# Eight transposed first tiles at both feed-forward openings, and a later convolution LayerNorm schedule

## The reference

```python
for l in range(2):
    h = rmsnorm(x, mix_norm_g[l])
    # layer 0: a, gate, p = split(h @ w_in)
    #   ya = silu(layernorm(depthwise_conv31(a * sigmoid(gate)) + b))
    #   yb = multi-scale pooling mixer of p
    # layer 1: Fourier mixer (2-D DFT) beside a gated spatial mixer
    x = x + mixer_l(h) @ w_out[l]
    h = rmsnorm(x, ffn_norm_g[l])
    x = x + (silu(h @ w_gate[l]) * (h @ w_up[l])) @ w_down[l]   # hidden width 2816
out = rmsnorm(x, final_norm_g)
```

## Time and profile before

| what | value |
|---|---|
| median of 3 runs | 2642.21 us (2639.93 to 2644.13) |
| profiled execution: span of the slowest core (core 4) | 2639.2 us |
| spans of the 8 cores in it | 2633.3 to 2639.2 us |
| busy share in the span, PE / DVE / ACT / POOL | 97% / 32% / 24% / 15% |
| mean granted TensorE clock, core 4 | 0.985 |

### The profile page before, as it was taken

One profiled execution on the slowest core, in us unless ns is written; L12 is line 12 of the kernel. 1 busy time (PEld: TensorE's weight loads), 2 busy tenths in 40 slices (PEclk: granted clock), 3 DMA queues, 4 the chain that ended last, 5 costly groups with the idle time before them and its releaser, 6 DMA issues.

```text
span 2639.2 us, 38782 instructions; the slowest of 8 cores (2633.3 to 2639.2 us)
## 1 busy us (share of the span) xinstructions
PE 2549.2 (97%) x12907; PEld 1205.6 (46%) x12907; DVE 835.2 (32%) x1278; ACT 626.3 (24%) x1090; POOL 404.1 (15%) x701
## 2 busy tenths in 40 slices
PE   6999799999999999999999997999999999999998
PEld 3447344444444444444444473444444444444443
DVE  3426443222222222221223673222222222222122
ACT  3434443122111111111132353121121111111111
POOL 2200132101110111011023531221011111100100
PEclk8999899999999999999999988999999999999999
DMA  7976579856664896455564157895366447644422
GB/s 172 233 159 141 132 130 185 157 152 128 125 139 127 141 160 147 122 79 81 144 122 120 17 91 170 143 172 108 114 130 124 112 112 136 117 116 104 74 47 96
DMA packets 324877, 335.09 MB, mean 127 GB/s; under 512 B 152768, under 2 KB 282704, under 8 KB 324560
## 3 DMA queue, kind: packets, MB, share of 16 engines
q0 software_dynamic: 122096, 118.40, 32.6%
q1 hardware_dynamic: 192944, 205.30, 27.9%
q10 hardware_dynamic: 9648, 8.92, 1.2%
HBM read 331.92 MB, written 83.89 MB: 158 GB/s over the span
## 4 chain that ended last, share of the span: by engine, by line
PE 91%; DMA 3%; DVE 2%; issue 1%; SPq 1%; POOL 1%; ACT 1%; DVEq 0%; POOLq 0%; ACTq 0%
PE ps L171 91%; SPq L185 1%; DMA BIG<-hbp 1%; DMA pdr<-pst 1%; DMA w_in<-ev_w_in 1%; DMA xin<-x 0%; DMA xres<-xr 0%; DVE vt L1184 0%; POOL rs L373 0%; POOL vn L1189 0%; DVE bst L1169 0%; DMA BIG<-hb 0%; DVE bst L855 0%; DVE mv L1172 0%; ACT vn L875 0%
## 5 line engine op out<-in xcount | busy, mean ns | idle before, releaser
L171 PE MATMUL ps<-BIG,wgu 128*128 128x512 bf16 x5632 | 1229.7, 380 | 15.4 <-DMA BIG<-hbp 15.4
L171 PEld LDWEIGHTS ps<-BIG,wgu 128*128 128x128 bf16 x5632 | 551.4, 98 | 680.7 <-issue 20.9
L171 PE MATMUL ps<-wd,gT 128*128 128x512 bf16 x2816 | 609.1, 379 | 0.0
L510 DVE TENSOR_TENSOR gT<-tmp,ps 128x512 bf16<-128x512 f32 x352 | 242.1, 688 | 838.7 <-PE ps L171 792.7
L171 PEld LDWEIGHTS ps<-wd,gT 128*128 128x128 bf16 x2816 | 275.5, 98 | 332.3
L508 ACT ACTIVATE tmp<-ps 128x512 f32<-128x512 f32 x352 | 208.9, 594 | 756.8 <-PE ps L171 724.5
L171 PE MATMUL ps<-w_in,BIG 128*128 128x512 bf16 (+1 forms) x1344 | 289.2, 375 | 8.0 <-ACT pst L422 4.7
L185 POOL DMA_DIRECT2D wgu<-ffn_wgu x176 | 134.5, 765 | 855.1 <-PE ps L171 826.5
L171 PE MATMUL ps<-w_out,BIG 128*128 128x512 bf16 x1024 | 233.2, 382 | 3.6 <-ACT BIG L902 1.5
L387 ACT ACTIVATE hb<-xr 128x1024 bf16<-128x1024 f32 x80 | 84.6, 1057 | 554.7 <-DVE xr L484 280.1
L171 PEld LDWEIGHTS ps<-w_in,BIG 128*128 128x128 bf16 x1344 | 132.0, 99 | 151.6 <-issue 14.7
(11 more groups left out here) (130 smaller groups left out, 1103.1 us busy)
## 6 DMA issues: line engine op xcount, KB each, us to landing
wgu<-ffn_wgu POOLq DMA_DIRECT2D x176, 512.0 KB, 7.1
xr<-xr SPq DMA_DIRECT2D x59, 512.0 KB, 4.0
xin<-x SPq DMA_DIRECT2D x32, 512.0 KB, 6.3
xr<-xres SPq DMA_DIRECT2D x32, 512.0 KB, 5.2
xnat<-xr SPq DMA_DIRECT2D x32, 512.0 KB, 3.7
out<-xr SPq DMA_DIRECT2D x31, 512.0 KB, 2.9
xr<-x SPq DMA_DIRECT2D x28, 512.0 KB, 7.6
xres<-xr SPq DMA_DIRECT2D x28, 512.0 KB, 5.1
```

The source lines that it names most:

```text
L171: ins = self.nc.tensor.matmul(o, lhsT=l, rhs=r, start=st, stop=sp)
L510: k.op(dve, lambda e: e.tensor_tensor(out=gT[:, j, tg * 512:(tg + 1) * 512], in0=tmp[:], in1=ps[:, bl[1], :], op=ALU.mult), reads=[d_tmp, ...
```

## The change

In `prologue`, the DMA transposes of tiles 0 to 2 go. All eight tiles go through `tr_pe`, each two tiles behind its projection: tiles 0 to 4 in the loop, tiles 5 to 7 before `up(0, 0)`, `up(1, 0)` and `up(2, 0)`. In layer 0 (`npre` is 2) the copies of tiles 1 and 3 are made on VectorE behind the residual add; the others, and all in layer 1, on ScalarE ahead of it. The loop also does tile 7's projection and add, and the scaling of tile 6. `pro` does nothing after a slice any more. `feed(99)` comes before `up(3, 0)`, at the same place in the order of the instructions as before.

In `bg0`, groups 4 to 7 get one part per slice and one group per two slices: stat at j = 1, 3, 5, 7, norm at j = 2, 4, 6, 8, silu at j = 3, 5, 7, 9. Before, group 4+n had stat and norm at j = n and silu at j = n+1. Groups 8 to 11 come one slice earlier (stat at 3, 5, 7, 9; norm at 4, 6, 8, 10). At an even slice the norm of group 8+n comes before the norm of group 5+n.

```diff
                 if t + len(op.xr.s) < 8:
                     op.load(t + len(op.xr.s))
-                if t < 3:
-                    op.nrm.tr(t)
-
-            for i in range(7):
+
+            for i in range(8):
                 op.mm(i, 1 if i < npre else None)
-                if i >= 5:
+                late = npre and i % 2
+                if 2 <= i < 7 and not late:
                     op.nrm.tr_pe(i - 2, ident, d_ident, 0)
                 op.add(i)
+                if 2 <= i < 7 and late:
+                    op.nrm.tr_pe(i - 2, ident, d_ident, 1)
                 if i:
                     scale(i - 1)
                 feed(i)
 
             def pro(j, after):
-                if not after:
-                    if j < 2:
-                        scale(6 + j)
+                if after:
                     return
+                if j == 0:
+                    scale(7)
                 if j < 3:
                     op.nrm.tr_pe(5 + j, ident, d_ident, 0)
-                if j == 0:
-                    op.mm(7)
-                    op.add(7)
-                if j == 2:
+                if j == 3:
                     feed(99)
                     op.xr = xr
@@
             for n in range(4):
-                if j == n:
+                if j == 2 * n + 3:
+                    ln_silu(4 + n)
+                if j == 2 * n + 2:
+                    ln_norm(4 + n)
+                if j == 2 * n + 4:
+                    ln_norm(8 + n)
+                if j == 2 * n + 1:
                     ln_stat(4 + n)
-                    ln_norm(4 + n)
-                if j == n + 1:
-                    ln_silu(4 + n)
-                if j == 2 * n + 4:
+                if j == 2 * n + 3:
                     ln_stat(8 + n)
-                if j == 2 * n + 5:
-                    ln_norm(8 + n)
```

## The result

The changed kernel takes 2610.94 us (median of 4 runs, 2608.98 to 2613.34), against 2642.21 us for the kernel before on the same chip. The ratio is 0.988, 95% interval 0.9864 to 0.9895. Forecast was 2613.0 us, range 2606 to 2621. The gain is about 31 us where 29 were forecast.

The account below looks back on a forecast made before the run. TensorE, 91% of the chain, bounds the kernel, so only its idling can be gained. 10.1 + 14.3 + 5.6 = 30.0 us, less 0.6, off 2639.2 us, plus 3.0 to the median: 2612.8, rounded to 2613 us; range 2606 to 2621.

Parts of the forecast that it names:

- Layer 0's opening: Tile 2's projection to `up(3, 0)`: 45.1 us falls to 35.0 us if nothing waits, saving 10.1 us.
- near miss: Layer 0's tiles copied on VectorE: scaling ends just as the next projection ends; put at nothing, up to 1 us.
- Layer 1's opening: First projection to `up(3, 0)`: 55.8 us falls to 41.5 us, saving 14.3 us.
- The LayerNorm groups: After `up(3, 0)` in layer 0: 6.5 us lost now, 0.3 us back at each of three slices, saving 5.6 us.
- PSUM rotation: PSUM pairs in layer 0's opening: each pair's last reader finishes 3 us or more early; three more pairs keep phase.
- From the span to the time: Whole kernel: 0.6 us off the gain for another core ending last, 3.0 us added from span to median.
- SP's queue: Layer 0's opening: tile 7's load there at 309 to 313, add due at 311; expected loss 0, worst about 1 us.
- B: Rival, chance 0.11: ScalarE and VectorE bound the opening, 6 us come back, 2619 us.
- C: Rival, chance 0.08: the LayerNorm wait moves to silu at slices 5, 7 and 9, up to 6.5 us; 2619 us.
- D: Rival, chance 0.03: crowded transfers, landings grow from 10 to 16 us, first slices wait 5 us per layer; 2623 us.
- E: Rival, chance 0.03: slower, TensorE granted 1.2 GHz throughout both openings, their 76.5 us of work doubles; 2689 us.

Follow-up runs that it names:

- l1_only: The kernel before with the new opening in layer 1 alone, layer 0 and the LayerNorm groups as before; ratio 0.9947 against the kernel before, 14.0 us.
- norm_swap: The changed kernel with the two LayerNorm passes of group 5+n put before the four of group 8+n at the even slices; ratio 0.988 against the kernel before.
- norm_late: The changed kernel with the LayerNorm passes of groups 8 to 11 one slice later (slices 5, 7, 9, 11); 2610.55 us.
- all_act: The changed kernel with the copies of tiles 1 and 3 in layer 0 on ScalarE ahead of the add too; 2611.28 us.

## Why the prediction was right, and where it wasn't

- **Layer 0's opening**, forecast 10.1 us, measured 9.6 on core 4. The missing half is 0.35 us ahead of tile 4's transposes and rounded unit prices. It is the near miss that the step had named, VectorE's 3.7 us against TensorE's 3.9 us, and had put at nothing.
- **Layer 1's opening**, forecast 14.3, measured 14.2 on core 4, and 14.0 by time alone. Counting work between two marks that exist on both sides gave it, including the part that comes from the clock. Core 4 had one of the long openings, and the median core gained 11.2 us. Taking the terms from the slowest core fits a metric that is the slowest core, though no step of mine argued that. (The 14.4 us in the expectation of `l1_only` took the group shown as x47 at its shown start.)
- **The LayerNorm groups**, forecast 5.6, measured 5.2 on core 4, and 6.1 (3 to 9) by time. The delays at three slices came to 1.3 us, where the step had 0.9. The cause I gave (silu's transposes wait for the last pass) is not what ends last, as `norm_swap` and `norm_late` show: the same queue on ScalarE also holds the bank of the next slice.
- **PSUM rotation**: the step said that three more pairs keep the rotation over three pairs in phase. That is true up to layer 1's start, where eight banks are used again and the phase is not kept. It was worth 1.5 us, by luck in our favour. This is the step that failed, and with it the sum would have been 2611.3 us.
- **From the span to the time**: the profiled span was forecast as 2609.8 us and came out as 2609.3. The 0.6 us for another core ending last was needed: core 4 fell to 2608.1 us, and core 2 ended last, 1.2 us above it. The 3.0 us from span to median were too much. The median is 1.6 us above the profiled span, and in each of the four runs the time is 1.3 to 1.5 us above the span of its slowest core. The rest of the 3.0 us was that the profiled execution of before was a short one. So of the 1.9 us by which 2610.94 lies under 2612.8, 1.4 come from this term.
- **SP's queue**: on core 4 tile 7's load was issued at 301.36, when tile 2's store had landed, and landed 8.2 us later, at 309.6. The add ran at 311.27. That is within the 309 to 313 of the step. On core 6 the load took 10.4 us and was late. VectorE's timeline, then PE's:

```profile
312.74 1.22 DVE L484 TENSOR_TENSOR xr<-xr,ps 128x1024 f32<-128x1024 f32 x1 [3.29 <-DMA xr<-x]
```

```profile
315.52 0.61 PE L171 MATMUL ps<-ident,hbp 128*128 128x128 bf16 x8 [0.52 <-ACT hbp L387]
```

The add came about 1.5 us late, and TensorE waited ahead of tile 6's transposes, so that this core's opening is 0.7 us longer than the others'. The step had said that 1.3 us would be covered, and at worst 1 us lost.

- **The rivals**: B fell with the waits in the openings (0.35 us, and 0.7 us more on core 6) and with `all_act`. C fell with 1.3 us in all at silu. D fell too: the first weights did land later (below), but PE has no wait for `wgu`, and the late `xr` cost 0.7 us on one core. E fell with clock 1.00 and 3.62 us per group.

## What to carry to other kernels

Where the chain leaves the bounding engine for a queue, price the stretch as a whole: take two marks that exist before and after, add up the bounding engine's work between them, and what is left is the most that a change which leaves this work as it is can give there. Do it on every core, since the slowest core may not be a typical one. Here the third DMA transpose at the head of a stage kept TensorE waiting 8.4 and 7.0 us on core 4, while a tile's transposes on TensorE, two tiles behind, cost 0.45 us and little more. When a change adds or removes PSUM allocations, follow the rotation to the next place where the number of banks changes, even a thousand microseconds on.

## What was not expected of the hardware

Taking the DMA transposes away made some transfers of layer 0's opening slower. The first weights landed in 14.7 us in the median on core 4 (12.2 before), and in 12.8 to 16.1 us on the eight cores (11.6 to 12.8 before). The residual stores landed in 8.6 us on core 4 (10.3 before). From tile 2's projection to `up(3, 0)` the core moved 232 GB/s, where it had 183 before, about the same bytes in less time. No wait of PE was for the weights. The same trace, DMA issues from 265 to 320 us:

```profile
wgu<-ffn_wgu POOLq DMA_DIRECT2D x4, 512.0 KB, 14.7
xres<-xr SPq DMA_DIRECT2D x4, 512.0 KB, 8.6
```
